# Alternating one expert's gate and up units with the other's down units in a mixture-of-experts trunk

## What is computed

```
def swiglu(h, wg, wu, wd):
    return (jax.nn.silu(h @ wg) * (h @ wu)) @ wd

def moe_top2(h, router, wg, wu, wd):      # 8 experts, 1024 -> 3584 -> 1024
    logits = (hf @ router).astype(jnp.float32)
    top_val, top_idx = lax.top_k(logits, TOP_K)
    gates = jax.nn.softmax(top_val, axis=-1)
    ...
    yb = lax.map(expert_block, (xb, block_exp))
    ys = yb.reshape(n_slots, d) * slot_gate[:, None].astype(h.dtype)
    y = jnp.zeros((t + 1, d), h.dtype).at[slot_tok].add(ys)[:t]
```

## Time and profile before

| | us |
|---|---|
| median of 3 runs | 1547.25 |
| lowest and highest | 1546.92, 1549.6 |
| the profiled execution | 1549.22 |
| its span, first to last instruction | 1547.4 |
| PE busy in it | 1466.4 (95%) |
| DVE busy | 1212.8 (78%) |
| ACT busy | 1039.0 (67%) |
| mean granted TensorE clock | 0.988 |

### The profile page before, as it was taken

The page is one execution under the profiler, slowest core; times in us unless marked ns, Lnnn a source line. Parts: engine busy times, 40 slices in busy tenths (PEclk is TensorE's granted clock), DMA queues, the critical chain, the costliest instruction groups (busy, mean ns, idle before and its releaser), DMA issues.

```text
span 1547.4 us, 18619 instructions
## 1 busy us (share of the span) xinstructions
PE 1466.4 (95%) x7062; PEld 1200.7 (78%) x7062; DVE 1212.8 (78%) x1126; ACT 1039.0 (67%) x980; POOL 6.3 (0%) x13
## 2 busy tenths in 40 slices
PE   6999999999899879999999999999999999999987
PEld 6877888888797668887778887778887778887766
DVE  5995555545579668879899879898879898979994
ACT  5565444434646457778887768887778877778874
POOL 0000000000000000000000000000000000000000
PEclk9999999999999979999999999999999999999998
DMA  9335555554250069999999999999999999999970
GB/s 341 119 105 173 189 184 190 190 191 154 82 190 2 0 254 408 389 350 396 390 403 374 371 353 377 392 395 392 355 357 374 394 398 381 377 344 375 393 289 28
DMA packets 143672, 441.83 MB, mean 286 GB/s; under 512 B 6928, under 2 KB 21296, under 8 KB 143584
## 3 DMA queue, kind: packets, MB, share of 16 engines
q1 hardware_dynamic: 142832, 438.24, 76.3%
q0 software_dynamic: 752, 2.39, 0.4%
HBM read 439.56 MB, written 1.05 MB: 285 GB/s over the span
## 4 chain that ended last, share of the span: by engine, by line
PE 72%; DVE 15%; ACT 7%; issue 5%; DMA 1%; DVEq 0%; SPq 0%; ACTq 0%
PE psum L512 17%; PE psum L514 17%; PE psum L513 17%; DVE w_lo L1687 9%; ACT w_hi L1230 5%; PE psum L958 4%; PE psum L959 4%; PE psum L560 3%; PE psum L1002 2%; PE psum L533 2%; PE psum L926 1%; PE psum L917 1%; PE psum L578 1%; PE psum L996 1%; DVE arena_a L1771 1%
## 5 line engine op out<-in xcount | busy, mean ns | idle before, releaser
L1687 DVE TENSOR_TENSOR w_lo<-ring,w_hi 128x2048 fp32r<-128x2048 f32 x406 | 921.5, 2286 | 246.7 <-ACT w_hi L1230 245.4
L1230 ACT ACTIVATE w_hi<-ring 128x2048 fp32r<-128x2048 f32 x406 | 773.2, 1912 | 285.5 <-PE psum L514 249.9
L514 PE MATMUL psum<-w_hi,hidden_b 128*128 128x512 f32 x560 | 219.1, 391 | 0.0
L958 PE MATMUL psum<-w_hi,xT_parts 128*128 128x512 f32 x448 | 193.3, 432 | 10.8 <-DVE w_lo L1687 10.7
L512 PE MATMUL psum<-w_hi,hidden_b 128*128 128x512 f32 x448 | 178.8, 399 | 5.4 <-DVE w_lo L1687 5.4
L959 PE MATMUL psum<-w_lo,xT_parts 128*128 128x512 f32 x448 | 175.9, 393 | 0.0
L513 PE MATMUL psum<-w_lo,hidden_b 128*128 128x512 f32 x448 | 175.1, 391 | 0.0
L512 PE MATMUL psum<-w_hi,xT_parts 128*128 128x512 f32 (+1 forms) x384 | 149.9, 390 | 5.3 <-DVE xT_parts L1694 2.8
L513 PE MATMUL psum<-w_lo,xT_parts 128*128 128x512 f32 (+1 forms) x384 | 149.2, 388 | 0.0
L514 PE MATMUL psum<-w_hi,xT_parts 128*128 128x512 f32 (+1 forms) x384 | 149.1, 388 | 0.0
L512 PE MATMUL psum<-w_hi,hidden_a 128*128 128x512 f32 x352 | 138.2, 393 | 0.0
(11 more groups left out here) (316 smaller groups left out, 1702.6 us busy)
## 6 DMA issues: line engine op xcount, KB each, us to landing
ring<-in_moe_w_gate SPq DMA_DIRECT2D x112, 1024.0 KB, 7.3
ring<-in_moe_w_up SPq DMA_DIRECT2D x112, 1024.0 KB, 7.6
ring<-in_moe_w_down SPq DMA_DIRECT2D x112, 1024.0 KB, 7.3
ring<-in_w_in SPq DMA_DIRECT2D x16, 1024.0 KB, 8.7
ring<-in_dense_w_gate SPq DMA_DIRECT2D x14, 1024.0 KB, 5.0
ring<-in_dense_w_up SPq DMA_DIRECT2D x14, 1024.0 KB, 5.2
ring<-in_dense_w_down SPq DMA_DIRECT2D x14, 1024.0 KB, 4.9
ring<-in_w_out SPq DMA_DIRECT2D x8, 1024.0 KB, 6.1
```

Source lines behind the costliest of these rows:

```text
L514: return mm(o, a[1], b[0], start=False, stop=final)
L958: mm(o, xl_hi_lo[kt], w[0][:, q, c], start=kt == 0, stop=False)
L1230: A(part(w_hi, g, sizes[g]), raw(g, sizes[g]), ACT.Copy).then_inc(hi_ready, 1)
L1687: V.tensor_tensor(part(w_lo, g, sizes[g]), raw(g, sizes[g]), f32(part(w_hi, g, sizes[g])), ALU.subtract).then_inc(lo_ready, 1)
```

## The change

The two experts of neighbouring steps run side by side. `heavy(i)` and `light(i)` become `heavy_up(i)` and `light_up(i)`: the 28 gate and up units of the one, with one down unit of the other after every second. So the stages' units run H H L (28 heavy up, 14 light down of the pair before) and L L H (28 light up, 14 heavy down). The first heavy_up has no partner, and `light_down` does the last light expert's down units alone at the end. `position` numbers the units in this order; loads, splits and semaphore counts follow it.

Hidden rows of both experts must live at once: the heavy ones stay in arena_a, the light ones lie in pieces of arena_b, xT and the small weights' space (`elT`). Light stationary tiles now hold high beside low once, and both light products use the same tile, which changes only which half of the output each partial product lands in; the fold adds the same four.

The scatters of both experts of a pair are done together in the next pair's light_up (`scatter_pair`, in banks 7, 4, 7, 4), the gather of the light expert moves to the end of heavy_up, that of the next heavy one from the light down units to the end of light_up, and with them take_light and take_heavy. The last pair's scatters lie in light_down and behind it. The second p load moves from the GpSimd queue to SP's.

```diff
-        elT = arena_a_r[:, 0:FKT * 3 * LIGHT].rearrange("p (k r s) -> p k r s", k=FKT, r=3)
...
+        elT = [buf[:, at:at + 2 * n * LIGHT].rearrange("p (k r s) -> p k r s", k=n, r=2) for buf, at, n in (
+            (arena_b_r, el_at0, 8), (xT_r, el_at1, 8), (small_r, 0, 8), (arena_b_r, el_at3, 4))]
...
+            up, half = c < DOWN0, EXPERT_UNITS if (c < DOWN0) == (k == 1) else 0
+            return half + (c // 2 * 3 + c % 2 if up else 3 * (c - DOWN0) + 2)
...
-                            mm(o, xl_hi_lo[kt], w[0][:, q, c], start=kt == 0, stop=False)
-                            last = mm(o, xl_lo_hi[kt], w[1][:, q, c], start=False, stop=kt == KT - 1)
+                            mm(o, xl_both[kt], w[0][:, q, cols], start=kt == 0, stop=False)
+                            last = mm(o, xl_both[kt], w[1][:, q, cols], start=False, stop=kt == KT - 1)
...
+            def scatter_pair(i, n):
+
+                if n == 0:
+                    pe.wait_ge(selgT_ready, step_done(i, 1))
+                    pe.wait_ge(ysb_ready, d_done(i, 1, 1))
+                    pe.wait_ge(hT_free, hT_done(i + 1, 0, 5))
+                elif n == 1:
+                    pe.wait_ge(hT_free, hT_done(i + 1, 0, 6))
+                else:
+                    pe.wait_ge(sc_free, sc_done(i, n - 2))
+                for k in range(2):
+                    scatter(k, n, SCATTER[n], k == 0, k == 1)
...
             def light_gT(i, ch, q0):
...
                     pe.wait_ge(g_free, ch_done(i, 1, ch))
                     if ch:
                         pe.wait_ge(sgT_ready, i * NCH + ch)
+                    elif isinstance(i, int) and i == 0:
+                        pe.wait_ge(hT_free, hT_done(i, 0, 6))
                     else:
-                        pe.wait_ge(sc_free, sc_done(i, 0))
+                        pe.wait_ge(sc_free, sc_done(i - 1, 3))
...
+            def light_up(i):
+
+                behind = not (isinstance(i, int) and i == 0)
+                for c in range(DOWN0):
+                    in_unit(i, 1, c)
+                    if behind and c in (1, 3, 4, 6):
+                        scatter_pair(i - 1, (1, 3, 4, 6).index(c))
...
+                    if c in (25, 26):
+                        for kt in range(4):
+                            gather(i + 1, 0, kt + 4 * (c - 25))
+                    if c % 2:
+                        down_unit(i, 0, c // 2)
+                    if c == 1:
+                        heavy_hidden(i, 6)
+                    elif c in (7, 15, 23):
+                        light_gT(i, c // 8, 0)
...
+                    if j == 0:
                         light_uT(i, NCH - 1, 0)
+                    elif j == 2:
+                        spread_gates(i, 0, tail=True)
+                    elif j == 4:
+                        spread_gates(i, 1)
...
-                        for r in (0, 2):
-                            last = A(elT[:, 8 * ch:8 * ch + n, r, :], v, ACT.Copy)
-                        last.then_inc(moe_h_hi, 1)
+                        A(elT[ch][:, :, 0, :], v, ACT.Copy).then_inc(light_h_hi, 1)
...
+                    for c in range(DOWN0):
+                        moe_split(ring_of(1, c) + SPLITS, i)
+                        if c == 2:
+                            heavy_rest(i, 6)
...
+                        elif c in (11, 19, 27):
+                            light_gated(i, c // 8 - 1)
...
+                        if c == 27:
+                            take_heavy(i + 1, 0)
+                        if behind and c in (2, 4, 5, 7):
+                            add_back(i - 1, (2, 4, 5, 7).index(c))
+                        if c % 2:
+                            moe_split(ring_of(0, DOWN0 + c // 2) + SPLITS, i)
+                    take_heavy(i + 1, 1)
```

More of the change, by code:

```diff
@@ L461, in trunk, with turn @@
         S0 = len(PARTED)
-        def turn(g):
-            return TURN[g] if g < N0 else S0 + g - N0
+        def turn(g, in_moe=False):
+            return S0 + g - N0 if in_moe or g >= N0 else TURN[g]
         def read_out(g):
@@ L1183, in _, with expert @@
-            for i in range(PAIRS - 1):
-                experts(i)
-            n_iter = sp.value_load(order[0:1, 0:1], min_val=PAIRS, max_val=2 * PAIRS)
-            with sp.Fori(PAIRS - 1, n_iter) as i:
-                experts(i)
+            def expert(at):
+                which = order[0:1, at:at + 1] if isinstance(at, int) else order[0:1, bass.ds(at, 1)]
+                ex = sp.value_load(which, min_val=0, max_val=NE - 1)
+                return tuple(w[0, bass.ds(ex, 1)].rearrange("a k n -> (a k) n") for w in (moe_g, moe_u, moe_d))
@@ new lines, in beside, with pair @@
+            def beside(i, k, up, down):
+                for c in range(DOWN0):
+                    sp.wait_ge(lo_ready, unit_of(i, k, c) - SLOTS + 1)
+                    load(ring_of(k, c), *expert_unit(*up, c))
+                    if c % 2:
+                        j = DOWN0 + c // 2
+                        sp.wait_ge(lo_ready, unit_of(i if k else i - 1, 1 - k, j) - SLOTS + 1)
+                        load(ring_of(1 - k, j), *expert_unit(*down, j))
+            def pair(i):
+                heavy, light_before = expert(i * 2 + 1), expert(i * 2)
+                beside(i, 0, heavy, light_before)
+                beside(i, 1, expert(i * 2 + 2), heavy)
@@ new lines, in _ @@
+            first = expert(1)
+            for c in range(DOWN0):
+                if c < SLOTS:
+                    sp.wait_ge(*read_out(N0 + c - SLOTS))
+                else:
+                    sp.wait_ge(lo_ready, unit_of(0, 0, c) - SLOTS + 1)
+                load(N0 + c, *expert_unit(*first, c))
+            beside(0, 1, expert(2), first)
+            for i in range(1, PAIRS - 1):
+                pair(i)
+            last_pair = sp.value_load(order[0:1, 0:1], min_val=PAIRS - 1, max_val=2 * PAIRS - 1)
@@ new lines, in _ @@
+            n_iter = last_pair + 1
+            with sp.Fori(PAIRS - 2, last_pair) as before:
+                pair(before + 1)
+            last = expert(last_pair * 2 + 2)
+            for j in range(DOWN_UNITS):
+                sp.wait_ge(lo_ready, tail_of(n_iter, j) - SLOTS + 1)
+                load(N0 - DOWN_UNITS + j, *expert_unit(*last, DOWN0 + j))
+                if j == SLOTS:
+                    sp.wait_ge(ysb_ready, d_done(n_iter - 1, 0, 1))
+                    sp.dma_start(ptok[1], p[1, 0].rearrange("(t p) c -> p t c", p=P)).then_inc(last_ptok_in, 16)
@@ L1605, in _ @@
+                    heavy_up(0)
+                    light_up(0)
+                    for i in range(1, PAIRS - 1):
+                        heavy_up(i)
+                        light_up(i)
+                    with act.Fori(PAIRS - 2, last_pair) as before:
+                        heavy_up(before + 1)
+                        light_up(before + 1)
+                    light_down(last_pair)
+                    h_done = [(*divmod(n, 2), (sc_free, sc_done(n_iter - 1, n))) for n in range(4)]
                 o = banks.filled(act, ("pT", L))
@@ L2237, in experts @@
+                heavy_up(0)
+                light_up(0)
+                for i in range(1, PAIRS - 1):
+                    heavy_up(i)
+                    light_up(i)
+                with dve.Fori(PAIRS - 2, last_pair) as before:
+                    heavy_up(before + 1)
+                    light_up(before + 1)
+                light_down(last_pair)
                 take_pT(DEPTH - 1)
                 for n in range(4):
-                    add_back(n_iter, n)
+                    add_back(n_iter - 1, n, LAST_SCATTER)
```

586 lines of the change are left out of this document (318 added, 268 removed).

## The result

The changed kernel takes 1606.93 us (median of 4 runs, 1604.39 to 1609.6), 1.0383 times the kernel before (95% interval 1.0363 to 1.0403): slower, as forecast, and by 59.7 us instead of 36.8. It is outside the range, which ended at 1600. The profiled execution took 1604.39 us, the least of the four. PE is busy for 17.3 us more than before (1483.7 against 1466.4), with the same 7062 products, transposes and gathers.

The account below looks back on a forecast made before the run. PE's work was taken as the bound, 222 us a pair, with waits added by queue order. Stages of 85.0 + 114.8 + 728.7 + 41.8 = 970.3 against 932.9 gave +37.4, forecast 1584 us; range 1548 to 1600.

Parts of the forecast that it names:

- The three named waits: New PE waits for short DVE instructions queued behind a split, in light_up and at its end: together 9.4 us a pair.
- (b): In light_up after light unit 7, the first gate transposes wait for the fourth addition back: 3.4 us, three times.
- (c): At the border to the next heavy_up, its first unit waits for take_heavy behind a split: 2.55 us, three times.
- (a): In light_up after light unit 3, the second scatter pair waits for heavy_rest 6 behind a split: 3.5 us, three times.
- The pair, 242.9: Each of three heavy_up and light_up pairs: 222.2 us of PE work plus 9.4 and 11.3 of waits.
- the clock: Rival, chance 0.13: PE falls to 1.2 GHz behind the nine named waits, 1.7 us each, 15 in all, 1599.
- the nine named waits: Waits (a), (b) and (c) in light_up and at its end, each coming three times: 3.5, 3.4 and 2.55 us.
- the last stage's waits of 5.4 and 3.3: In light_down, the gates' transposes wait for light_gated behind a split (5.4 us), the second ones for selg (3.3).
- Small waits, 11.3 a pair: Short PE waits at light_up's entry (0.95 us), in its middle (5.75) and in heavy_up (4.6).
- The mix wins: Rival, chance 0.11: across the expert stages small waits vanish and the named ones at most halve; -22 us, 1525.
- Stationary tile 0: One stationary tile for both light products saves no PE time: taken as 0, at most 1 us a pair.
- DMA 0: Loads: the same 84 a pair, slower stages ask for less, so no effect on time.

Follow-up runs that it names:

- all moves: Changed kernel with three DVE moves ahead of splits, ACT's silus and copies behind splits, last-stage light_silu, light_rest, light_gated one unit earlier: 1550.05 us, ratio 1.001.
- the second version: Kernel with all moves, plus scatter pairs and two add_backs moved, build_sel behind unit 16's split, last-stage build_selg ahead of its split: 1545.53 us, ratio 0.9987.

## Why the prediction was wrong, by its steps

*Direction and mechanism: right.* The three named waits stood where the walk through the queues put them, at 3.1 to 3.5, 3.2 and 2.5 us (forecast 3.5, 3.4, 2.55), for the instructions named. When its instruction was put ahead of the split, (b) and (c) went, and (a) fell from 9.8 us in all to 2.9.

*The pair, 242.9: right as a sum of work and waits.* With PE kept busy during the named waits it is 243.5, and the clock is 1.00. (The 109.7 for heavy_up is 1.5 more than the items named for it; a lot of light transposes, 0.9, and the gates, 0.6, both in the 222, would make it up.)

*The failed step: the clock was a rival (0.13), not a term.* The prediction priced it correctly (1.7 us a fall, from the earlier trace rows) and named the waits that could bring it, then left it at 0 in the sum and capped the range at its value, 1600. Two things were missed. The row for it was in hand: 2.89 us of wait had been followed by a fall, 1.44 had not the earlier trace rows, and six of the nine named waits were forecast at 3.4 or 3.5, beyond the first. By the nearest row the likeliest case was a fall behind most of them. And the count stopped at nine, while the last stage's waits of 5.4 and 3.3 are of the same kind. Measured: 11 pieces of half clock, 18.7 us; the eight behind the named waits, when they were kept away, gave 13.9. With 18.7 in the sum the forecast would have been 1603, and the range with its end at 1600 would have missed even that. The Trainium skill (TensorE: Matmul & The Clock Gate, Part 1: The HAM clock gate) says that an idle array falls to 1.2 GHz; the trace agrees for most waits over 2.2 us, though not for all (the one of 3.2 that ends at 1422, the one of 2.5 that ends at 766.5, and one in the kernel with take_heavy moved). So the page alone did not settle which of the nine waits would bring a fall, and "by it this would be the case" said more than it states.

*The rest of the account.* Expert part 992.0 - 970.3 = 21.7. Of it 18.7 is the clock. The first heavy_up took 2.0 more than forecast, which is a wait of 1.8 at the first light unit that I had not walked; the first light_up 2.1 more, for which I have no single cause; the three pairs without their falls 1.2 more (743.5 - 13.6 = 729.9); the last stage without its falls 2.3 less (44.6 - 5.1 = 39.5, forecast 41.8). Outside the expert part the profiled execution is 3.9 shorter than that of before (612.4 against 616.3), and it has 5 pieces at half clock there against 8 (without the very end of the span, where PE is done): up to 5.1 us by 1.7 each. The stretches in which they differ, kernel before:

```profile
500.00:562.60 62.60, 50.11 (x258) 42.18 (x256) 37.40 (x98) 27.55 (x56) 0.70 (x1) 0.84 0.12 41
1497.60:1540.00 42.40, 37.42 (x166) 29.61 (x164) 22.30 (x30) 21.76 (x38) 0.58 (x1) 0.96 0.04 15
```

And the kernel after:

```profile
500.00:562.60 62.60, 47.53 (x257) 39.80 (x256) 39.21 (x97) 29.14 (x57) 0.00 (x0) 0.89 0.13 51
1554.60:1597.00 42.40, 35.88 (x166) 28.04 (x165) 22.07 (x31) 23.16 (x43) 0.55 (x1) 1.00 0.04 13
```

That the number of these pieces changes where the code does not, no run explains. The profiled executions differ by 55.2 us and the medians by 59.7, because the one of the changed kernel lay 2.5 under its median and the one of before 2.0 above.

*Small waits, 11.3 a pair: mechanism shown, size in part.* Moving ACT's silus and copies took about 4 of them a pair. What is left after all moves is 9 a pair over the sum of PE's work.

*The mix wins: not as changed.* The bound named for it, 11.4 us of waits a pair, was right as a bound: with the queues mended (the second version) the pair is 2.3 under that of before. The rest of the gain stays in small waits. All three pairs take 695.5 us by the starts of their first products, where three of before take 699.5; the first heavy_up, the first light_up and the last stage take 235.1 together, where before's remaining pair took 233.6, and so give 1.5 of the 4.0 back.

*Stationary tile 0: right*, by the run on the kernel before. The rule of the Trainium skill (same page, Part 2: What happens when you issue a matmul), that one load can serve many products, is not what this kernel's products do: each still has its load. ACT's copies of light hidden rows were halved as forecast, from 32 (L1539 before) to 16 (L1663). *DMA 0*: nothing speaks against it. In the slower stages its share fell to 0.93 and in the mended ones it is 1.00, so it follows PE.

## What to carry to other kernels

When work of two streams is interleaved on one engine, the short instructions that free banks and buffers decide, more than the mix: write each queue out, and put an instruction that somebody waits for ahead of a long one whose own input comes late. Price a new wait of PE at its length plus the half-clock time that the trace shows behind waits of that length, and count every such wait, the ends included. Where a wait can't be removed, products with no use issued in front of it can keep the clock, as they did behind the nine waits here; all of them ended before their wait did, and longer ones were not tried.

## What the hardware showed beyond expectation

- Equal waits do not fall equally. Waits (b), 3.2 us each, brought one piece of half clock, two in a row and none in one execution of the changed kernel. Moving one instruction elsewhere changed the count at untouched waits (11 pieces to 6 where two or three should have gone). What decides it was not settled. The runs of some of these kernels also spread more than those of before (with the rest moved 8.7 us, 1595.21 to 1603.91, beside 5.2 of before on the same chip), but with the copies moved, where the trace has the most pieces, 12, they spread by 1.6; so the falls are not shown to be the reason.
- Three fp32 products of 512 columns took 2.74 us at a granted clock of 1.00: 6 records that start 0.43 apart, so 0.86 for a product, against 0.227 for one in fp32r.
